# Dense host layout for weights and tokens, conv transfers in another order, and a last tile in column halves: a two-layer conv/gMLP step on eight cores

## The reference

```
for i in range(2):
    mod = silu(c) @ w_ada[i] + b_ada[i]                  # six rows of D
    h = rmsnorm(x) * (1 + sc1) + sh1
    layer 0: a = h @ w_pw1; z = a[:D] * sigmoid(a[D:])
             y = causal depthwise conv of width 31 over z
             out = silu(layernorm(y)) @ w_pw2
    layer 1: u, v = gelu(h @ w_in); v = layernorm(v)
             out = (u * chunk_mix(v)) @ w_out            # chunks of 128 tokens
    x += g1 * out
    h = rmsnorm(x) * (1 + sc2) + sh2
    x += g2 * ((silu(h @ w_gate) * (h @ w_up)) @ w_down)
return rmsnorm(x)
```

## Time and profile before

| | |
|---|---|
| time, median of 3 runs | 1997.21 us (1996.36 to 1998.49) |
| the profiled execution | 2000.2 us; span of its slowest core (core 7) 1998.7 us, so 1.5 us lie around the span |
| spans of the eight cores | 1968.8 to 1998.7 us |
| PE busy | 1687.6 us (84% of the span) |
| DVE, ACT, POOL busy | 983.5, 591.1, 83.8 us |
| granted TensorE clock, mean | 0.933 of full |
| moved by DMA | 162.37 MB; read from memory 214.07 MB |

### The profile page before, as it was taken

How to read it: one execution, slowest core, us unless ns; L and a number is a source line. 1 busy time by engine, 2 the same in 40 slices (tenths; PEclk the granted TensorE clock), 3 DMA queues, 4 the chain that set the end, 5 groups by cost and what they waited for, 6 DMA issues and landing times.

```text
span 1998.7 us, 27744 instructions; the slowest of 8 cores (1968.8 to 1998.7 us)
## 1 busy us (share of the span) xinstructions
PE 1687.6 (84%) x10144; PEld 812.6 (41%) x10144; DVE 983.5 (49%) x1598; ACT 591.1 (30%) x831; POOL 83.8 (4%) x112
## 2 busy tenths in 40 slices
PE   1497863885799999999887988997789999999985
PEld 0134532532344444444344444443334444444442
DVE  1346671475453435444565556564634433453456
ACT  1335551473521010103333232423542111111132
POOL 1000010000000000000000000001000000000000
PEclk8689986887899999999998999999989999999997
DMA  9864598113432305422055753346240302240012
GB/s 169 144 188 72 82 170 204 53 42 126 64 43 49 53 12 85 64 43 43 13 115 109 120 155 85 106 98 160 101 85 1 64 1 32 41 78 10 1 65 105
DMA packets 106601, 162.37 MB, mean 81 GB/s; under 512 B 3264, under 2 KB 80832, under 8 KB 102210
## 3 DMA queue, kind: packets, MB, share of 16 engines
q0 software_dynamic: 79696, 104.48, 30.6%
q1 hardware_dynamic: 26772, 56.12, 8.9%
HBM read 214.07 MB, written 27.72 MB: 121 GB/s over the span
## 4 chain that ended last, share of the span: by engine, by line
PE 65%; DVE 11%; DMA 9%; ACT 8%; issue 6%; DVEq 0%; ACTq 0%; SPq 0%; POOLq 0%
PE PS L443 61%; PE PS L452 4%; DMA Wada<-w_ada 2%; DMA X<-xp 2%; ACT L464 1%; DMA scr_b<-BBR 1%; ACT HF L464 1%; DMA scr_z<-ZT 1%; DVE ST L1376 1%; DVE X L480 1%; DVE gTM L480 1%; DVE gRS L486 1%; DVE fRS L486 1%; ACT HB L464 1%; ACT H L464 1%
## 5 line engine op out<-in xcount | busy, mean ns | idle before, releaser
L443 PE MATMUL PS<-HF,Wg 128*128 128x512 bf16 x1408 | 342.6, 387 | 32.7 <-ACT HF L464 31.9
L443 PE MATMUL PS<-HF,Wu 128*128 128x512 bf16 x1408 | 334.9, 381 | 0.0
L443 PE MATMUL PS<-HID,Wd 128*128 128x512 bf16 x1408 | 314.9, 380 | 13.2 <-DVE HID L468 11.8
L468 DVE TENSOR_TENSOR HID<-SGT,PS 128x512 bf16<-128x512 f32 x176 | 120.7, 687 | 407.8 <-PE PS L443 375.6
L480 DVE SCALAR_TENSOR_TENSOR X<-PS,MOD,X 128x512 f32<-128x512 f32 x384 | 261.8, 744 | 104.1 <-PE PS L443 104.0
L464 ACT ACTIVATE SGT<-PS 128x512 f32<-128x512 f32 x176 | 104.9, 597 | 692.8 <-PE PS L443 632.3
L443 PEld LDWEIGHTS PS<-HF,Wg 128*128 128x128 bf16 x1408 | 138.8, 99 | 203.5 <-issue 46.4
L443 PEld LDWEIGHTS PS<-HID,Wd 128*128 128x128 bf16 x1408 | 136.2, 98 | 180.6 <-issue 20.9
L443 PEld LDWEIGHTS PS<-HF,Wu 128*128 128x128 bf16 x1408 | 138.4, 98 | 169.3 <-issue 5.9
L443 PE MATMUL PS<-HB,Wpw 128*128 128x512 bf16 x512 | 123.0, 401 | 36.2 <-DMA Wpw<-w_pw 22.6
L443 PE MATMUL PS<-Wv,H 128*128 128x512 bf16 x512 | 123.8, 385 | 19.1 <-DVE MOD L468 13.7
(11 more groups left out here) (181 smaller groups left out, 1438.9 us busy)
## 6 DMA issues: line engine op xcount, KB each, us to landing
Wada<-w_ada POOLq DMA_DIRECT2D x24, 1024.0 KB, 11.1
Wgu<-scr_wu POOLq DMA_DIRECT2D x12, 1024.0 KB, 5.3
Wgo<-scr_wo POOLq DMA_DIRECT2D x12, 1024.0 KB, 5.5
X<-xp SPq DMA_DIRECT2D x10, 1024.0 KB, 13.9
Wg<-w_gate POOLq DMA_DIRECT2D x10, 1024.0 KB, 11.1
Wu<-w_up POOLq DMA_DIRECT2D x10, 1024.0 KB, 12.5
Wd<-w_down POOLq DMA_DIRECT2D x10, 1024.0 KB, 9.7
yp<-X SPq DMA_DIRECT2D x16, 512.0 KB, 2.9
```

The source lines that it names most:

```text
L443: ins = pe.matmul(out, lhsT=l, rhs=r, start=(first and i == 0), stop=(last and i == n - 1))
L468: return S.comp('dve', lambda v, o=out, a=in0, b=in1, op=op: v.tensor_tensor(out=o, in0=a, in1=b, op=op), reads, writes)
```

## The change

- The host stores each weight piece as one dense block, [128, 4096] float32, 16 KB per partition; the arena loads it as one run per partition. The scratch tensors are flat too.
- xp and yp become [4 tiles, 128, 8, 512].
- In `ln_gen`, `back(h, 0)` is issued after chunk 3; the reload of X leaves `silu` and goes into `finish_half(h)`, behind `back(h, 1)`, as four transfers of 1 MB. `finish_half(0)` stands ahead of the six steps of `c_gen(1)`, `finish_half(1)` behind `ln_gen(1)`. BBC becomes two dense tiles of 8 KB per partition. The copy `cssc` moves from behind the conv's first half to behind `finish_half(1)`.
- The last tile of the last unit does its down product, final norm and output by halves of 256 columns (`last_down`), after the rest of the task f2.

```diff
-    xp_d = din("xp", [128, KC, SEQ])
+    xp_d = din("xp", [NTI, 128, KC, NT])
-    w_ada_d = din("w_ada", [2, D, 6 * D])
+    w_ada_d = din("w_ada", [2, 6, 2, 128, KC * 512])
...
-            return wrows(w_ada_d[l], 0, KC, j * D + h * 512, 512), KC, 512
+            return w_ada_d[l, j, h], KC, 512
...
-            S.dma('pool', v, src, reads=rd, writes=[buf], sem='A%d' % k)
+            S.dma('pool', flat, src, reads=rd, writes=[buf], sem='A%d' % k)
...
-                if h == 1 and c % 4 == 3:
-                    back(1, c // 4)
-                if c % 2 == 1:
-                    S.dma('sp', X[:, c - 1:c + 1, h * 1024:(h + 1) * 1024], xp_d[:, c - 1:c + 1, h * 1024:(h + 1) * 1024],
-                          writes=ta.xb[c - 1:c + 1] + tb.xb[c - 1:c + 1])
+                if c == 3:
+                    back(h, 0)
...
+        def finish_half(h):
+            back(h, 1)
+            for T in (pt[2 * h], pt[2 * h + 1]):
+                for c in (0, 4):
+                    S.dma('sp', X[:, c:c + 4, T.t0:T.t0 + NT], xp_d[T.idx, :, c:c + 4, :], writes=T.xb[c:c + 4])
...
-        for h in range(4):
-            AR.release(('pw1', h))
-        back(0, 0)
-        for _ in ln0:
-            pass
-        back(0, 1)
-        S.dma('sp', csp_d[:, :, :], ZL[:, :, :], reads=[B_ZL])
-        steps(c1, 6)
-        S.dma('sp', cssc_d[:, :, :], sc_d[:, 1:CTX, :])
+        for _ in ln0:
+            pass
+        finish_half(0)
+        steps(c1, 4)
+        for h in range(4):
+            AR.release(('pw1', h))
+        steps(c1, 2)
+        S.dma('sp', csp_d[:, :, :], ZL[:, :, :], reads=[B_ZL])
...
+    def last_down(T, l, wd, bd, HID, B_HID, n):
+        W = NT // 2
+        BG.finish('f%d' % (NTI - 2))
...
+        down(0, 0)
+        down(0, 4)
+        down(1, 0)
+        stats(0)
+        down(1, 4)
+        out(0)
+        stats(1)
+        out(1)
```

More of the change, by code:

```diff
@@ L210, in build_program @@
     oq_d = din("oq", [128, 128])
-    w_ada_d = din("w_ada", [2, D, 6 * D])
[L212 to L220, removed]
+    w_ada_d = din("w_ada", [2, 6, 2, 128, KC * 512])
+    w_pw1_d = din("w_pw1", [4, 128, KC * 512])
+    w_pw2_d = din("w_pw2", [2, 128, KC * 512])
+    w_v_d = din("w_v", [4, 128, 2 * E])
+    w_u_d = din("w_u", [4, 128, KC * 512])
+    w_out_d = din("w_out", [4, 128, EC * 256])
+    w_gate_d = [din("w_gate%d" % u, [2, 128, KC * n * 128]) for u, n in enumerate(UNIT_CHUNKS)]
+    w_up_d = [din("w_up%d" % u, [2, 128, KC * n * 128]) for u, n in enumerate(UNIT_CHUNKS)]
+    w_down_d = [din("w_down%d" % u, [2, 128, n * D]) for u, n in enumerate(UNIT_CHUNKS)]
+    yp_d = dout("yp", [NTI, 128, KC, NT])
     ys_d = dout("ys", [128, KC, NS])
@@ L531, in build_program @@
     for c in (0, 4):
-        S.dma('sp', X[:, c:c + 4, 0:NT], xp_d[:, c:c + 4, 0:NT], writes=B_X[0][c:c + 4])
+        S.dma('sp', X[:, c:c + 4, 0:NT], xp_d[0, :, c:c + 4, :], writes=B_X[0][c:c + 4])
     memset(ONESB[:, :], 1.0, [B_ID])
@@ L743, in ffn_tile @@
             tick()
-        if release:
+        if u == len(FUNITS) - 1 and T.idx == NTI - 1:
             AR.release(('g', l, u))
@@ L764, in ffn_tile, with down, stats, out @@
             mid(1)
+    def last_down(T, l, wd, bd, HID, B_HID, n):
+        W = NT // 2
+        BG.finish('f%d' % (NTI - 2))
+        RSTD, B_RS = place("fRS", KBX(53.5), [128, 2, W], parts=2)
+        SQ, B_SQ = place("fSQ", KBX(57.5), [128, 2, KC, W], BF16, parts=4)
+        b_x = [[Buf("XT%d_%d" % (m, h)) for h in range(2)] for m in range(KC)]
+        for m in range(KC):
+            for h in range(2):
+                b_x[m][h].w = T.xb[m].w
+                b_x[m][h].r = list(T.xb[m].r)
+        cols = [slice(h * W, (h + 1) * W) for h in range(2)]
+        def down(h, m0):
+            banks = [ps_next() for _ in range(4)]
+            for mi in range(4):
+                m = m0 + mi
+                mm_group(PS[:, banks[mi], 0:W], [(wd[:, hc, m * 128:(m + 1) * 128], HID[:, hc, cols[h]]) for hc in range(n)],
+                         [bd, B_HID], [B_PS[banks[mi]]])
+                stt(T.xc[m][:, cols[h]], PS[:, banks[mi], 0:W], modcol(l, 5, m), T.xc[m][:, cols[h]], ALU.mult, ALU.add,
+                    [B_PS[banks[mi]], B_MOD[l][5], b_x[m][h]], [b_x[m][h]])
+            act(SQ[:, h, m0:m0 + 4, :], T.x3[:, m0:m0 + 4, cols[h]], AF.Square, [b_x[m][h] for m in range(m0, m0 + 4)],
+                [B_SQ[2 * h + m0 // 4]])
+        def stats(h):
+            b = ps_next()
+            mm_group(PS[:, b, 0:W], [(ONESB[:, :], SQ[:, h, c, :]) for c in range(KC)], [B_SQ[2 * h:2 * h + 2], B_ID],
+                     [B_PS[b]])
+            act(RSTD[:, h, :], PS[:, b, 0:W], AF.Sqrt, [B_PS[b]], [B_RS[h]], bias=EPS, scale=1.0 / D)
+            recip(RSTD[:, h, :], RSTD[:, h, :], [B_RS[h]], [B_RS[h]])
+        def out(h):
+            for c in range(KC):
+                stt(T.xc[c][:, cols[h]], T.xc[c][:, cols[h]], ppc('fng', c), RSTD[:, h, :], ALU.mult, ALU.mult,
+                    [b_x[c][h], B_PP, B_RS[h]], [b_x[c][h]])
+                if c % 2 == 1:
+                    S.dma('sp', yp_d[T.idx, :, c - 1:c + 1, cols[h]], T.x3[:, c - 1:c + 1, cols[h]],
+                          reads=[b_x[c - 1][h], b_x[c][h]])
+        down(0, 0)
[6 more added lines that the diff above has]
+        out(1)
     def ffn_sample(l, u, T, st, part):
@@ L813, in ffn_phase @@
                     last_tile(tiles[i])
+                if lastu and l == 1 and i == NTI - 1:
+                    pass
                 if u > 0 or i not in done:
@@ L822, in ffn_phase @@
                 AR.release((k, l, u))
-        if last_tile is not None:
+        if last_tile is not None and l == 0:
             last_tile(tiles[-1])
@@ L1018, in back @@
             R_, B_R = BBR[h]
[L1019 to L1022, removed]
+            C_, b_ = place("BBC", KBX((0 if h == 0 else 28.5) + 8 * k), [128, 4, 4, 256], BF16)
+            BBC.setdefault(h, []).append((C_, b_))
             bd = BD[2 * h + k]
@@ L1026, in back @@
                   R_[:, :, 4 * k:4 * k + 4, :].rearrange("p b c s -> p b (c s)"), reads=[B_R[k]], writes=[b_bd])
-            S.dma('sp', C_[:, :, 4 * k:4 * k + 4, :].rearrange("p q c s -> p q (c s)"), bd, reads=[b_bd], writes=[B_C[k]])
+            S.dma('sp', C_.rearrange("p q c s -> p q (c s)"), bd, reads=[b_bd], writes=[b_])
         TTP = []
         def e_gen(T):
-            C_, B_C = BBC[T.idx // 2]
+            CB = BBC[T.idx // 2]
             TT2 = [place("TT", KBX(78.5 + 2 * i), [128, NT]) for i in range(2)] if T.idx % 2 == 0 else TTP[0]
@@ L1039, in e_gen @@
                 mm_group(PS[:, b, :].rearrange("p (q s) -> p q s", q=4),
-                         [(v[:, kc, o:o + 128], C_[:, :, kc, s0:s0 + 128]) for kc in range(KC)],
-                         [wb] + B_C, [B_PS[b]])
+                         [(v[:, kc, o:o + 128], CB[kc // 4][0][:, :, kc % 4, s0:s0 + 128]) for kc in range(KC)],
+                         [wb, CB[0][1], CB[1][1]], [B_PS[b]])
                 TT_, B_TT = TT2[m % 2]
@@ L1125, in conv_phase @@
             pass
[L1126 removed]
+        S.dma('sp', pt[1].x3, xp_d[1, :, :, :], reads=[B_MOD[0][0]], writes=B_X[1])
         ada_q = [(0, j, h) for j in (2, 3, 4, 5) for h in (0, 1)]
@@ L1134, in conv_phase @@
         BG.finish('n1')
-        S.dma('sp', pt[2].x3, xp_d[:, :, 2 * NT:3 * NT], writes=B_X[2])
+        S.dma('sp', pt[2].x3, xp_d[2, :, :, :], writes=B_X[2])
         steps(b1, 4)
@@ L1142, in conv_phase @@
             steps(sg, 1)
-        S.dma('sp', pt[3].x3, xp_d[:, :, 3 * NT:4 * NT], writes=B_X[3])
+        S.dma('sp', pt[3].x3, xp_d[3, :, :, :], writes=B_X[3])
         BG.add('n2', norm_task(pt[2], l, 1, hb_dst(pt[2]), tmn))
```

62 lines of the change are left out of this document (37 added, 25 removed).

## The result

The changed kernel takes 1979.6 us (median of 4 runs, 1978.9 to 1982.9) against 1996.8 for the kernel before in the same measurement: a ratio of 0.9916, 95% interval 0.9899 to 0.9933. That is 17 us faster where 42 were forecast. The sign held and the range held it by a hair; the size was off by more than half. In some executions the cores of one die show a lower granted clock and take some per cent longer; all ratios here leave these out.

What follows compares the result with a forecast made beforehand. PE, busy 84% of the span, was taken to lose time to waits at start, conv, gMLP and tail. Gains of 3 + 27 + 9 + 3 = 42 us from 1997.2 gave 1955; 8-in-10 range 1922 to 1980.

Steps and rivals of the forecast that it cites:

- Density brings little rate, and packets take turns: Weight transfers: dense layout buys little rate (330 GB/s read where crowded, 400 elsewhere); SP's small packets each wait for a big one.
- rule of equal counts: DMA: where both queues are busy, they finish packets one for one, 777 and 777 in the profile before.
- rival (a): Big packets don't hold SP back: conv 48, start 8, the rest as forecast, 68 us gained, 1929; chance 19%.
- Start: Up to the conv: tile 0 later at about 49.5, tile 1 at about 75; 3 us gained, ends -3 and +10.
- Tile 1, requested at about 60, lands at about 75 against 78.1: Start: the second token tile arrives at about 75 us instead of 78.1, giving 3 us gained taken together.
- Conv: Hops without reloads ahead: `e_gen` starts at about 326 instead of 354.8; 27 us gained, ends 18 and 48.
- first ZR there at 285, e_gen right behind the conv steps at about 304: Conv's upper end: with no sharing penalty, ZR at 285 and `e_gen` at about 304, 48 us gained.
- 2 to 5 us each: Conv: time for each later hop (BBC, second z, its ZR, second scr_b), about 0.5 to 1 MB at some 400 GB/s, plus 2.
- gMLP: Weight waits of 18.2 us shrink: 2.5 for each of three waits, 2 on the scratch read; 9 us gained, ends 4 and 15.
- Tail: DVE's end takes 23.5 us against 26.0 and the last store is half as big; 3 us gained, ends 0 and 7.
- Rival (b): Hops get dearer through memory sharing or bundled packets: conv 15, gMLP 4, start -3, tail 2; 18 us gained, 1979; chance 16%.
- Rival (c): Dense 16 KB rows stream slower: at factor 0.81 it costs 18 us, still gaining 24; at 0.6, 2006; chance 6%.

Runs made afterwards that it cites:

- e1: The changed kernel with the weight pieces strided as in the kernel before (1 KB packets); 1967.5 us, ratio 0.9836 to the kernel before.
- e5: The kernel before with only the layout of xp and yp changed to dense tiles of 512 tokens; ratio 0.9962 to the kernel before.
- e11: The changed kernel, all pieces in 16 KB runs, with the four pieces after w_pw1 held until both BBC have landed; ratio 0.9793 to the kernel before.
- e7: The changed kernel with strided weight pieces and the four pieces after w_pw1 held until both BBC have landed; ratio 0.9753 to the kernel before.

## Why the prediction was half right

**Density brings little rate, and packets take turns: right.** The rule of equal counts held for unlike packets (605 and 607, 1040 and 1032), so rival (a) fell. Tile 0 came at 52.2 where 49.5 was worked out; the first product at 72.1 (median over the cores 70.7) where 69 to 70 was.

**Start: wrong by 11 us; the step that failed is "Tile 1, requested at about 60, lands at about 75 against 78.1".** On core 1 it was asked for at 65 and landed at 90.4, in the median over the cores at 63.3 and 85.8. So 3 of the 11 us are a later request, which tile 0 had pushed back, and the rest is the load: 22.5 us (21.6 to 25.5) where 15 were worked out. The kernel before had already shown how long it takes there, 29.8 us (median). Only some 3 of the 22.5 are the price of the big packets, for e1 with small ones takes 19.3. In short, tile 1 was late because tile 0 was, and its load was never as short as the sum had it. The toll on tile 0 itself was right. Two terms hid behind each other: the big packets cost 18 us of start (e1 to after), and tokens in tiles, which the sum gave nothing, brought 12 back (e5).

**Conv: mechanism right, size off (12 to 14 us instead of 27).** The term that failed is the chain of hops without any sharing, "first ZR there at 285, e_gen right behind the conv steps at about 304". From the issue of the first half's z write (272.7) the forecast has `e_gen` 31.3 us later without sharing and 53.3 with it (326), so 22.0 for the backlog. Measured, as medians over the cores, it is 40.2 us without (e11) and 62.4 with (after): 22.2 for the backlog. The sharing, then, was priced right to the microsecond, in the total, and the hops' own time was 9 us too low: "2 to 5 us each" holds for a write alone (4.3 to 5.4 us in the second half of the conv), but in the chain each write goes out beside a read and takes 7 to 8. Another 5 us come from the core: the chain was worked out from core 7, the slowest, with 82.1 us before, where the median core had 76.8. Together that is what lies between the 28.8 us that this stretch was to lose and the 14.4 that it lost. Without sharing the conv steps were to set the time of `e_gen`; in e11 PE still waits 1.9 us for ZR and 4.3 for BBC, so the hops set it.

Hop by hop the agreement is looser. Medians over the cores: the first z write took 16.7 us where 13.3 were worked out (286 less 272.7), the ZR read with the first scr_b write 23.4 where 22 were, and from there to `e_gen` it was 21.5 where 18 were. On core 1 it was 25.5, 17.3 and 23.8.

**gMLP: a little too much credited.** 9 us were forecast; measured are 3.2 by the table and 6.2 by the cores' own stretches. PE's waits for gMLP weights fell from 18.2 to 10.9 (7.1 + 3.8) on the slowest core, 7 us. The first Wgo pieces are no longer waited for there, but the read of scr_wo still is, for 7.1 us instead of 6.8, and that was one of the terms (2 us).

**Tail: right** (23.6 us for 23.5; the stretch -3.0). **The FFN: right**, nothing gained (-0.2 us by the cores' own stretches).

Rival (b) named 1979, the time that was measured, with hops made dearer. Part of that is what happened: its conv of 15 us is nearly the measured one. But it charged the start 3 us of loss, where 7.9 were lost, and laid the cost on full-rate pieces or bundles. The hops are dearer than worked out with those pieces held back as well (e11), and the backlog costs as much with small packets (e1, e7). Its number is closer than its reason. Rival (c), dense blocks streaming slower, is out: the start reads at 336 GB/s, where it had 328 times 0.81.

## What to carry to other kernels

Before widening a queue's runs, ask who shares the engines with it: where queues take turns by the packet, big packets on one are a tax on every small one of the other, and it falls on the transfers that something waits for. Take the time of such a transfer from what it took before in the same place, not from its bytes alone: tile 1 had taken 30 us where 15 were worked out, and a write beside a read of its own chain 7 where it takes 4 alone. If a chain of small hops lies beside a prefetch that nobody needs yet, hold the prefetch until the chain is through: here that took 20 to 24 us off the conv, more than the whole change brought, and cost nothing that a mark shows.

## What was not expected of the hardware

- Two layouts of the same 2 KB runs differ: with tokens 8 KB apart the core moved 186 GB/s from 4 to 30 us, with dense tiles 202 (the same weights beside them), and the kernel went to 0.9962 [0.9938, 0.9986]. The cause is open.
- A write of 1.05 MB on SP's queue lands 4.2 us after its issue with nothing beside it (e7, at 392 us). Half a microsecond behind a 0.56 MB read on the same queue it takes 7.0 us (at 272 us), with no weight piece beside either: the two together move 1.61 MB in those 7 us.
- Sharing hurt the small transfers by as much with 1 KB packets on the other queue as with 8 KB packets when summed over the four hops (medians 54.3 and 55.1 us, 32.8 with the pieces held). Which hop pays depends on the packet size; the sum fell only with the pieces held. At the start, where the transfers are longer, the size does matter: 18 us.
